# Eleven and twelve products with dropped results on TensorE, ahead of the third decay level and ahead of the gated output's turns

## The reference, cut to what matters

```
def chunk_gated_linear(q, k, v, logf):      # C = 64 rows a chunk, 4 chunks, 8 heads of 128
    def step(S, inp):
        qc, kc, vc, gc = inp
        b = jnp.cumsum(gc, axis=-2)
        decay = jnp.exp(jnp.where(mask[:, :, None], b[..., :, None, :] - b[..., None, :, :], -jnp.inf))
        attn = jnp.einsum('bhtsk,bhsk->bhts', decay * qc[..., :, None, :], kc)
        o = jnp.einsum('bhts,bhsv->bhtv', attn, vc) + jnp.einsum('bhtk,bhkv->bhtv', qc * jnp.exp(b), S)
        ...
h = x @ w_in;  q, f, i, g = split(h)
o = rms_norm(o, g_norm) * silu(g)
return o.reshape(B, T, D) @ w_o
```

## Time and profile before

| what | us |
|---|---|
| median of 3 runs | 1041.49 |
| lowest, highest of them | 1040.15, 1042.12 |
| the profiled execution | 1040.88 |
| its span, start of the first to end of the last instruction | 1039.2 |
| TensorE busy in it | 977.8 |
| VectorE, ScalarE, GpSimd busy | 653.0, 474.3, 152.8 |

### The profile page before, as it was taken

How to read it: one execution, slowest core, us unless ns; L and a number is a source line. 1 busy time by engine, 2 the same in 40 slices (tenths; PEclk the granted TensorE clock), 3 DMA queues, 4 the chain that set the end, 5 groups by cost and what they waited for, 6 DMA issues and landing times. The chain is left out here.

```text
span 1039.2 us, 11948 instructions
## 1 busy us (share of the span) xinstructions
PE 977.8 (94%) x4727; PEld 809.4 (78%) x4727; DVE 653.0 (63%) x1004; ACT 474.3 (46%) x587; POOL 152.8 (15%) x142
## 2 busy tenths in 40 slices
PE   7888999999998989898999999989989999999995
PEld 5666788888886878896788888868867878888883
DVE  4678666455467838887855455585346466767674
ACT  4554343434343474433343434344464455565652
POOL 2120000000004927621100000010000011212120
PEclk9899999999999999888999999989999999999997
DMA  8880465655647543212655655548530356555620
GB/s 281 174 149 1 141 204 183 202 175 190 200 165 246 187 137 120 84 41 81 223 187 179 201 182 183 165 158 294 186 107 2 107 196 181 183 187 178 188 97 40
DMA packets 103511, 165.89 MB, mean 160 GB/s; under 512 B 3931, under 2 KB 72570, under 8 KB 103456
## 3 DMA queue, kind: packets, MB, share of 16 engines
q1 hardware_dynamic: 99968, 152.61, 44.4%
q0 software_dynamic: 3488, 12.53, 5.4%
HBM read 160.93 MB, written 4.19 MB: 159 GB/s over the span
## 5 line engine op out<-in xcount | busy, mean ns | idle before, releaser
L593 DVE TENSOR_TENSOR wlo<-raw,whi 128x2048 fp32r<-128x2048 f32 (+1 forms) x139 | 318.9, 2313 | 109.8 <-ACT whi L584 109.8
L584 ACT ACTIVATE whi<-raw 128x2048 fp32r<-128x2048 f32 (+1 forms) x141 | 266.0, 1906 | 48.8 <-PE PA L1609 36.8
L1607 PE MATMUL PG<-whi,xlo 128*128 128x512 f32 x608 | 243.6, 401 | 5.7 <-DVE wlo L1201 2.9
L1609 PE MATMUL PG<-whi,xhi 128*128 128x512 f32 x608 | 239.0, 393 | 0.0
L1608 PE MATMUL PG<-wlo,xhi 128*128 128x512 f32 x608 | 238.8, 393 | 0.0
L1607 PEld LDWEIGHTS PG<-whi,xlo 128*128 128x128 f32 x608 | 115.7, 190 | 30.6 <-DVE wlo L1201 3.3
L1607 PE MATMUL PA<-whi,xlo 128*128 128x512 f32 (+1 forms) x312 | 123.4, 395 | 12.3 <-DVE xlo L1534 5.0
L1609 PEld LDWEIGHTS PG<-whi,xhi 128*128 128x128 f32 x608 | 115.5, 190 | 24.8
L1608 PEld LDWEIGHTS PG<-wlo,xhi 128*128 128x128 f32 x608 | 115.8, 191 | 22.8
L1608 PE MATMUL PA<-wlo,xhi 128*128 128x512 f32 (+1 forms) x312 | 121.0, 388 | 0.0
L1609 PE MATMUL PA<-whi,xhi 128*128 128x512 f32 (+1 forms) x312 | 120.9, 388 | 0.0
(11 more groups left out here) (254 smaller groups left out, 1142.7 us busy)
## 6 DMA issues: line engine op xcount, KB each, us to landing
raw<-in_ffn_w_gate SPq DMA_DIRECT2D x44, 512.0 KB, 4.0
raw<-in_ffn_w_up SPq DMA_DIRECT2D x44, 512.0 KB, 5.0
raw<-in_ffn_w_down SPq DMA_DIRECT2D x22, 1024.0 KB, 4.9
raw<-in_w_up SPq DMA_DIRECT2D x44, 512.0 KB, 4.7
raw<-in_hgrn_w_in SPq DMA_DIRECT2D x16, 1024.0 KB, 5.3
raw<-in_w_qkv SPq DMA_DIRECT2D x12, 1024.0 KB, 5.1
raw<-in_w_down SPq DMA_DIRECT2D x11, 1024.0 KB, 4.8
raw<-in_att_w_o SPq DMA_DIRECT2D x4, 1024.0 KB, 5.6
```

The source lines that it names most:

```text
L584: nc.scalar.activation(whi[:, g, 0:n_], raw[:, s, 0:n_], ACT.Copy).then_inc(S("w_hi"), 1)
L593: nc.vector.tensor_tensor(wlo[:, s, 0:n_], raw[:, s, 0:n_], whi[:, g, 0:n_].bitcast(F32), ALU.subtract).then_inc(S("w_lo"), 1)
L1607: mm(dst, xl[:, k, rows], whi[:, g, cols], start=first, stop=False)
L1609: return mm(dst, xh[:, k, rows], whi[:, g, cols], start=False, stop=last_)
```

## The change

A function `filler(dst, n_)` is added to TensorE's program and called twice: with 11 products into TB between `up(U_H + 12, ...)` and `level(2)`, and with 12 products into PG ahead of `turn_rows("ho", ...)`. Each reads two slices of `xhi`, waits for no semaphore and raises none, and nothing reads its result before the bank is written anew.

```
+            def filler(dst, n_):
+
+                for _ in range(n_):
+                    mm(dst, xhi[:, 0, 0:P], flat(xhi[:, 0:2, :]), start=True, stop=True)
+
...
             up(U_H + 12, lambda r: PG[:, r, :], lambda: level(1), 4)
+            filler(TB[:, 0, :], 11)
             level(2)
...
                 last.then_inc(S("ho"), 1)
+            filler(PG[:, 0, :], 12)
             turn_rows("ho", oh, lambda g: pe.wait_ge(S("oh"), g + 1))
```

## The result

The changed kernel's median was 1048.17 us (1043.15 to 1049.27, 5 executions), that of the kernel before beside it 1041.84 us (1040.15 to 1045.67, 5 executions). The ratio is 1.0054, 95% interval 1.0033 to 1.0075: slower, and above the range that was given (1040.4 to 1045.3). Three later comparisons of the same two kernels, with 12 executions of the changed one each, gave 1.0020 (1.0005 to 1.0035), 1.0010 (0.9993 to 1.0028) and 1.0022 (1.0003 to 1.0041). So in the three later comparisons the change costs some 2 us, and the first five executions lay 3 us above what came later.

A forecast was written before the change was run, and what follows sets the result against it. TensorE, busy 977.8 of 1039.2 us, was taken to bound, the path running from level 2 over VectorE to level 3. 1040.88 + 2.5 + 0 - 0.8 = 1042.6 us, median 1043.2; range 1040.4 to 1045.3.

The forecast's parts named there:

- three things that the prediction named as signs of being wrong: Gap ahead of level 3 shrunk by over 0.5 us, clock 1.00 in level 4, or transposes waiting for the twelve.
- The eleven products: Ahead of level 2 on TensorE: they push both sides of the gap and are paid in full, +2.5 us.
- the two numbers that the prediction named: VectorE's idle time ahead of its first level 2 copy, 2.7 us; idle gap ahead of level 3, 2.6 to 2.7.
- The clock in levels 3 and 4: Levels 3 and 4 on TensorE: the clock falls again as before, 0, with -5.2 and +1.8 us kept as bounds.
- The slower case: Levels 3 and 4: low clock right from level 3's start, +1.8 us; part of a rival with chance 0.13.
- the faster: Levels 3 and 4: no clock fall, VectorE binds, level 5 starts sooner, -5.2 us; rival's chance 0.10.
- The twelve products: Ahead of the gated output's turns: hidden in TensorE's wait, full clock behind them, -0.8 us.
- the 1.6 us: Most the twelve could gain: 0.7 us at the other eight transposes, 0.9 us at the output projection's first four products.
- a gap of 1.29 us ahead of transposes brought no fall: Evidence from 61.0 to 66.7 us, clock 1.00, that the 1.49 us gap between second and third group might do no harm.
- Rival 1: At the turns: the twelve bring nothing, the eleven are still paid, 1044.0 us; chance 0.24.
- The sum: Whole kernel: 1040.88 + 2.5 + 0 - 0.8 = 1042.6 us, median 1043.2 us, 0.16% more, read as no change.
- the forecast's own spread: Whole kernel: spread of the main forecast (chance 0.46); its upper half gave 0.02 to slower by over 0.2%.

The follow-up runs named there:

- e4: Eleven products moved into the idle gap ahead of level 3, twelve left out, against the kernel before: median 1035.55 us, ratio 0.9947.
- e1: The changed kernel again, no edit, beside the kernel before: median 1044.35 us over 12 executions.
- e2: Only the eleven products ahead of level 2, twelve left out, against the kernel before: ratio 1.0026, mean 1044.5 us.
- e3: Only the twelve products ahead of the gated output's turns, eleven left out, against the kernel before: ratio 0.9988, mean 1040.8 us.
- e13: The change plus six products between the second and third group of the turns, against the kernel before: median 1041.35 us, ratio 1.0000.
- e15: The changed kernel again, no edit, timed for the fourth time beside the kernel before: median 1044.25 us (1039.68 to 1048.02).
- e10: The changed kernel, no edit, one more profiled execution to find a slow one: 1046.25 us.
- e12: The kernel before, no edit, one more profiled execution: 1042.54 us.
- e16: The twelve products alone once more, eleven left out, against the kernel before: ratio 0.9987, mean 1041.0 us.

## Why the prediction was wrong, and where it was right

None of the three things that the prediction named as signs of being wrong came: the gap ahead of level 3 did not shrink, the clock was low in level 4, and the transposes came 3.13 us behind the last product with the values, as before. What failed are the size of one term and, above all, the range.

**The eleven products, +2.5 us: right.** 18.09 became 20.59 us in every trace, +4.99 for twice as many, and the comparison of the eleven alone gives +2.7 us. Nothing absorbed it. VectorE's idle time of 2.70 us and the unchanged gap of 2.67 us are the two numbers that the prediction named.

**The clock in levels 3 and 4, 0: right.** From level 3 to level 5 it was 19.15 to 19.21 us in five of six profiles of the changed kernel, and 19.2 before. The slower case (+1.6 measured, +1.8 forecast as its bound) came once, the faster never; its price of 5.2 us was that of e4 (5.1), which needs the gap filled.

**The twelve products, -0.8 us: too large by the traces, open by the means.** That they are hidden was right (3.13 us before and after). What failed is the step that took half of the 1.6 us because "a gap of 1.29 us ahead of transposes brought no fall", and that let the gap at issue stay at 1.49 us. It was 1.49 us at the low clock; with the first groups at full clock TensorE is through sooner and the gap grows to 1.95 us, since VectorE sets when the third group may start. In all six profiles of the change the clock fell behind it, and the turns took 15.26 to 15.30 us, against 15.25 and 15.85 before: 0 to 0.6 us.

Rival 1, with its 0.24, is what the traces of the change show, and its 1044.0 us lies within 1.3 us of the three later medians. The executions leave it open: the twelve alone were 0.9 and 1.0 us under before by the means, beside the eleven 0.3 us (e1 against e2), and none of this is clear of noise. The rule of the Trainium skill ("TensorE: Matmul & The Clock Gate", part 4), that transposes do not count as work that brings the full clock, gave the same 0. But e3 and e13 had all sixteen transposes at the full clock, and 1.5 us came back there. Whether transposes hold the clock by themselves these runs do not tell, since the twelve stand ahead of them and in e13 the six between them.

**The sum.** By the traces the change costs 2.5 us where the clock falls in the same places, and the three later comparisons give +2.5, +1.0 and +2.4 us by the means. The forecast of +1.7 us lies among them; that it "reads as no change" does not hold: two of the three intervals exclude 1, and that of the first comparison too. With 0 for the twelve the sum would have been 1044.0 us, still inside the range and far under 1048.17.

**The range: this is the step that put the prediction outside.** It was made of the mechanisms' prices at the two places of the change, as if a median showed them bare. For everything else it had next to nothing: 0.02 for the upper half of the forecast's own spread, and no term for low clock at other places. But single executions spread over nearly 7 us before (1039.3 to 1046.1) and over 9.6 us after (1039.7 to 1049.3), and a median of five moves by 1 to 2 us with it. Three executions of before, within 2 us of each other, hid that. The traces show what the spread is made of: the time up to level 0, ahead of the change, lies between 401.3 and 405.0 us, by where and for how long the clock is low there; levels 3 to 5 and the values add 1.6 us each or do not. With the largest value of each column that bears on the changed kernel, it comes to 405.0 + 20.6 + 11.9 + 20.8 + 9.9 (level 5 to the values) + 10.0 + 15.3 + 544.8 = 1038.3 us, and 9.8 us for what lies outside these marks (1043.15 less the sum of its own row, with 9.9 for level 5 to the values) make 1048.1. That is where the slowest of e15 lie.

**What stays open.** The executions at 1049.0 and 1049.3 us lie above that sum. And four of the first five were over 1045.5 us, when 9 of the later 36 were; none of those four was profiled. Their mean clock says that the excess is in the main low clock and no fixed cost: three of them had 0.965 and took 1048.2 to 1049.3 us, and the five of the later 36 that had 0.965 took 1047.7 to 1048.4. But five drawn at random out of all 41 have a mean as high as 1047.0 in less than one case in a hundred. So it was a rare draw, or something was different at that time; nothing here tells which. Nor is it shown that the added products never run at the low clock: no execution over 1046.25 us was profiled. It may be that they did: where the mean clock was 0.972 the changed kernel took 2.7 us more than the one before (1043.1, 5 executions; 1040.4, 19), and where it was 0.965 it took 3.8 us more (1048.3, 8; 1044.5, 9).

## What to carry to other kernels

In these runs products with dropped results helped only inside an idle gap. Their place is to be read from the gap's own row: the same eleven cost 2.5 us one stage ahead of it and gave 5.5 us back inside it (e4). Where another engine sets when TensorE may go on, a faster TensorE makes the gap longer (1.49 us became 1.95), so look for the next one before counting the gain. When the clock falls in places that differ from execution to execution, ask for the spread of single executions before a range is drawn from the mechanisms alone.

## What the runs showed of the hardware

The 64 products of 64 columns of levels 3 and 4 ran at the full clock for 7.36 us in a row when the gap ahead of them was filled (e4). With the 2.67 us open they took 12.33 us, for the most part at 1.2 GHz. Transposes with 0.55 us of idle time between them kept the full clock (e13), and with 1.95 us in one profile of ten (e3). And the place of a fall is not the program's alone: behind the same gap it came 0.1 us (e10), 1.4 us (e12) and 2.4 us (e13) after the start of level 3. What a low-clock stretch costs can be read from the executions of the kernel before beside e1: seven with a mean clock of 0.972 took 1040.4 us in the mean, three with 0.963 took 1044.6. The 0.009 of 1040 us are 9.4 us of full clock, or 18.7 us more at the low clock, so by these ten a us of it cost 0.22 us (an estimate). A straight line through all 97 executions of before that stood beside e1 to e16 gives 0.27 us, and one through the 36 later ones of the changed kernel 0.33 us. A 128x512 product took 0.46 us at 1.2 GHz and 0.23 us at 2.4, so the price would be 0.5 us if TensorE bound everywhere. The rest probably lay where TensorE waits anyway, which no run here separates.
